# Two experts of a pair spread over interleaved groups of 32 partitions in a mixture-of-experts stage

## The reference, cut to what matters

```
g_idx   = top-1 of 4 groups;  e_idx = top-2 of the 8 experts in that group      # 2 of 32 experts for each token
gate    = softmax prob of the group * softmax over the two selected logits
for each expert e, for its rows xb:   y = (silu(xb @ w_gate[e]) * (xb @ w_up[e])) @ w_down[e]
out[token] += gate * y ;   x = x + out ;   return rmsnorm(x)
```

```
44 50 40 25 15 34 20 12 28 14 21 24 21 25 32 29 | 89 43 53 51 35 47 40 14 7 30 37 29 11 31 48 25
```

## Time and profile before

| | |
|---|---|
| median of 3 runs | 1301.31 us (1301.28 to 1301.44) |
| profiled execution | 1302.32 us, of which the span is 1300.0 us |
| TensorE busy, in the span | 1267.6 us (98%) |
| VectorE / ScalarE / GpSimd busy | 613.1 / 460.4 / 535.5 us |
| moved by DMA | 211.38 MB, mean 163 GB/s |
| mean granted TensorE clock | 0.994 of full speed |

### The profile page before, as it was taken

How to read it: one execution, slowest core, us unless ns; L and a number is a source line. 1 busy time by engine, 2 the same in 40 slices (tenths; PEclk the granted TensorE clock), 3 DMA queues, 4 the chain that set the end, 5 groups by cost and what they waited for, 6 DMA issues and landing times.

```text
span 1300.0 us, 18634 instructions
## 1 busy us (share of the span) xinstructions
PE 1267.6 (98%) x6670; PEld 968.7 (75%) x6670; DVE 613.1 (47%) x1162; ACT 460.4 (35%) x770; POOL 535.5 (41%) x685
## 2 busy tenths in 40 slices
PE   8999999999999999999999999999999999999986
PEld 6767777787888888888888788777888875555552
DVE  4868768725542422222225765757243265222225
ACT  5657534435434324133144534145322210000102
POOL 4633323334555655555545664424644211121100
PEclk9999999999999999999999999999999999999999
DMA  7422222112334433434333333312426989999995
GB/s 221 107 65 56 66 58 66 50 49 81 98 96 113 131 97 97 130 98 129 97 98 114 97 93 85 83 49 67 128 81 268 362 323 394 424 421 424 424 423 240
DMA packets 212157, 211.38 MB, mean 163 GB/s; under 512 B 31903, under 2 KB 193425, under 8 KB 200817
## 3 DMA queue, kind: packets, MB, share of 16 engines
q1 hardware_dynamic: 203104, 200.25, 45.8%
q0 software_dynamic: 5184, 8.29, 1.7%
q10 hardware_dynamic: 3796, 1.86, 0.5%
HBM read 205.76 MB, written 16.78 MB: 171 GB/s over the span
## 4 chain that ended last, share of the span: by engine, by line
issue 39%; POOL 31%; PE 26%; DMA 1%; DVE 1%; POOLq 0%; ACT 0%; SPq 0%; DVEq 0%; ACTq 0%
POOL wlo L661 31%; PE bank L2287 8%; PE bank L2304 4%; PE bank L1915 3%; PE bank L1917 3%; PE bank L1916 3%; PE side L1945 2%; DMA y<-y_rows 1%; PE bank L1956 1%; DMA y_rows<-xe,tabi 1%; PE side L1917 1%; PE side L1915 1%; PE side L1916 1%; PE side L2203 1%; PE bank L2419 0%
## 5 line engine op out<-in xcount | busy, mean ns | idle before, releaser
L661 POOL TENSOR_TENSOR wlo<-raw,whi 128x256 fp32r<-128x256 f32 x644 | 498.2, 805 | 524.4 <-ACT whi L785 524.2
L1916 PE MATMUL bank<-actB_lo,whi 128*128 128x512 f32 x608 | 236.7, 389 | 0.0
L1915 PE MATMUL bank<-actB_hi,whi 128*128 128x512 f32 x576 | 227.7, 395 | 0.5 <-POOL wlo L661 0.5
L1917 PE MATMUL bank<-actB_hi,wlo 128*128 128x512 f32 x576 | 224.4, 390 | 0.0
L785 ACT ACTIVATE whi<-raw 128x1024 fp32r<-128x1024 f32 x161 | 169.0, 1051 | 151.8 <-PE bank L1917 124.9
L1915 PE MATMUL bank<-actA_hi,whi 128*128 128x512 f32 x400 | 157.3, 393 | 0.6 <-DVE actA_lo L1201 0.6
L1916 PE MATMUL bank<-actA_lo,whi 128*128 128x512 f32 x400 | 156.1, 390 | 0.0
L1917 PE MATMUL bank<-actA_hi,wlo 128*128 128x512 f32 x400 | 156.1, 390 | 0.0
L2287 PE MATMUL bank<-gu,xeT 128*64 128x256 f32 x1088 | 127.7, 384 | 4.7 <-issue 2.2
L1916 PEld LDWEIGHTS bank<-actB_lo,whi 128*128 128x128 f32 x608 | 114.2, 188 | 24.1 <-issue 1.0
L1915 PEld LDWEIGHTS bank<-actB_hi,whi 128*128 128x128 f32 x576 | 108.1, 188 | 25.9 <-issue 2.3
(11 more groups left out here) (433 smaller groups left out, 1653.0 us busy)
## 6 DMA issues: line engine op xcount, KB each, us to landing
dn<-in_w_exp_down SPq DMA_DIRECT2D x32, 1024.0 KB, 16.0
raw<-in_w_in SPq DMA_DIRECT2D x57, 512.0 KB, 3.8
gu<-in_w_exp_gate SPq DMA_DIRECT2D x28, 1024.0 KB
gu<-in_w_exp_up SPq DMA_DIRECT2D x28, 1024.0 KB
raw<-in_w_up SPq DMA_DIRECT2D x32, 512.0 KB, 3.9
raw<-in_w_down SPq DMA_DIRECT2D x32, 512.0 KB, 3.6
raw<-in_w_out SPq DMA_DIRECT2D x16, 512.0 KB, 3.7
raw<-in_w_in SPq DMA_DIRECT2D x16, 256.0 KB, 3.1
```

The costliest lines, as they stand in the source:

```text
L661: ins = nc.gpsimd.tensor_tensor(wlo[:, slot, at], raw[:, slot, at], whi[:, slot, at].bitcast(F32), ALU.subtract)
L1915: mm(b[:, :], w_hi, hi[:, k, :], start=first, stop=False)
L1916: mm(b[:, :], w_hi, lo[:, k, :], start=False, stop=False)
L1917: ins = mm(b[:, :], w_lo, hi[:, k, :], start=False, stop=last)
```

## The change

1. The places of the experts of a unit are laid on partitions by groups of 32: expert 0's places 0 to 31 on partitions 0 to 31 and its places 32 to 63 on partitions 64 to 95, expert 1's on 32 to 63 and on 96 to 127 (`QUADRANTS`, `PLACES_OF`). Row numbers, targets and output scales are copied to these partitions in four pieces, where one instruction did it.
2. `rank_at` is filled otherwise: ranks 16o to 16o+15 go one to each of the 16 groups of four neighbouring places, upwards for even o and downwards for odd o.
3. The transposes of the rows write their columns back in the experts' order (`by_expert`), so gates, ups and `hid` stay as they were.
4. The downs are done in four groups of 32 columns, twice as many instructions of half the width.

```diff
+QUADRANTS = ((0, 0), (1, ROWS), (0, 32), (1, ROWS + 32))
+PLACES_OF = tuple((slice(32 * c, 32 * (c + 1)), slice(at, at + 32)) for c, (h, at) in enumerate(QUADRANTS))
+LAST_PLACES = PLACES_OF[-1][0]
+def by_expert(x):
+    return x.rearrange("p (h o s) -> p o h s", h=2, s=32)
...
-            ranks = const("iota")[:, 0:ROWS].rearrange("p (j b) -> p b j", b=8)
-            groups = rank_at.rearrange("p (b o) -> p b o", o=8)
-            for b in range(0, 8, 2):
-                chain(v.tensor_copy(groups[:, b:b + 2, b:8], ranks[:, b:b + 2, 0:8 - b]))
-                if b:
-                    chain(v.tensor_copy(groups[:, b:b + 2, 0:b], ranks[:, b:b + 2, 8 - b:8]))
+            ranks = const("iota")[:, 0:ROWS].rearrange("p (o e) -> p e o", e=16)
+            groups = rank_at.rearrange("p (e o) -> p e o", o=4)
+            for o in range(4):
+                if o % 2 == 0:
+                    chain(v.tensor_copy(groups[:, :, o:o + 1], ranks[:, :, o:o + 1]))
+                else:
+                    chain(v.tensor_scalar(groups[:, :, o:o + 1], ranks[:, :, o:o + 1], -1.0, float(32 * o + 15), ALU.mult, ALU.add))
...
-            chain(v.tensor_scalar(tabi[:, 1, 0:EXTRA_AT], bank[1][:, 0:EXTRA_AT], float(SKIP), None, ALU.add), S("rows_ready"))
+            for to, of in PLACES_OF:
+                ins = v.tensor_scalar(tabi[to, 1, 0:EXTRA_AT], bank[1][of, 0:EXTRA_AT], float(SKIP), None, ALU.add)
+                chain(ins, S("rows_ready") if to == LAST_PLACES else None)
...
-                chain(v.tensor_copy(slotv[:, :, FIRST], bank[2][:, EXTRA_AT:3 * EXTRA_AT].rearrange("p (n c) -> p n c", n=2)),
-                      S("values_listed"))
-                chain(v.tensor_scalar(tabi[:, 0, FIRST], bank[2][:, 0:EXTRA_AT], float(SKIP), None, ALU.add), S("slots_ready"))
+                chain(v.tensor_copy(slotv[:, 0, FIRST], bank[2][:, EXTRA_AT:2 * EXTRA_AT]), S("values_listed"))
+                for to, of in PLACES_OF:
+                    chain(v.tensor_copy(slotv[to, 1, FIRST], bank[2][of, 2 * EXTRA_AT:3 * EXTRA_AT]))
+                for to, of in PLACES_OF:
+                    ins = v.tensor_scalar(tabi[to, 0, FIRST], bank[2][of, 0:EXTRA_AT], float(SKIP), None, ALU.add)
+                    chain(ins, S("slots_ready") if to == LAST_PLACES else None)
...
-                    chain(v.tensor_tensor(tabi[rows, 1, to], slot, back, ALU.add))
-                    chain(v.tensor_copy(tabi[rows, 0, to], slot))
-                    chain(v.tensor_copy(slotv[rows, :, to], table[:, 1:3, :]), S("over_listed") if rows == LOW_ROWS else None)
+                    chain(v.tensor_tensor(back, slot, back, ALU.add))
+                    chain(v.tensor_copy(slotv[rows, 0, to], table[:, 1, :]))
+                    for at, of_ in PLACES_OF if rows == slice(0, P) else ((LOW_ROWS, LOW_ROWS),):
+                        chain(v.tensor_copy(tabi[at, 1, to], prod[of_, 0, EVENS:EVENS + of.stop - of.start]))
+                        chain(v.tensor_copy(tabi[at, 0, to], prod[of_, 0, 0:of.stop - of.start]))
+                        chain(v.tensor_copy(slotv[at, 1, to], late_table(of_, of)[:, 2, :]),
+                              S("over_listed") if rows == LOW_ROWS else None)
...
-                    ins = turn(side[k // 4][:, (k % 4) * P:(k % 4 + 1) * P], xe[:, n_x, :].rearrange("s (p j) -> s j p", j=NK)[:, k, :])
+                    ins = turn(by_expert(side[k // 4][:, (k % 4) * P:(k % 4 + 1) * P]), xe[:, n_x, :].rearrange("s (p j) -> s j p", j=NK)[:, k, :])
...
-                        for h, w in enumerate(weights):
-                            ins = mm(bank[2 + n][ROWS * h:ROWS * (h + 1), :],
-                                     hidT[:, j, k * P + ROWS * h:k * P + ROWS * (h + 1)],
-                                     w[:, k, n * L:(n + 1) * L], start=k == 0, stop=k == 1)
+                        for c, (h, at) in enumerate(QUADRANTS):
+                            ins = mm(bank[2 + n][32 * c:32 * (c + 1), :], hidT[:, j, k * P + at:k * P + at + 32],
+                                     weights[h][:, k, n * L:(n + 1) * L], start=k == 0, stop=k == 1)
```

More of the change, by code:

```diff
@@ L2402, in _ @@
                 for k in range(2):
[L2403 to L2406, removed]
+                    for c, (h, at) in enumerate(QUADRANTS):
+                        ins = mm(bank[2 + n][32 * c:32 * (c + 1), :], hidT[:, LAST_E % 2, k * P + at:k * P + at + 32],
+                                 dn[places_of(LAST_E)[h] % D_BUFS][:, k, n * L:(n + 1) * L], start=k == 0, stop=k == 1)
                 ins.then_inc(S("last_down_done"), 1)
```

## The result

The kernel after the change takes 1304.12 us (median of 20 runs, 1301.87 to 1309.10), the kernel before in the same comparison 1301.57 us (20 runs, 1300.46 to 1303.74). The ratio is 1.0022, with a 95% interval of 1.0013 to 1.0032: 0.22% slower, just past what the measurement tells from no change, 1.5 us above the forecast of 1302.6 and inside its range. The runs after scatter more than those before.

What follows compares the result with a forecast made beforehand. Full DMA engines, half ending late, were taken to set the end, with TensorE close behind. DMA summed to -2.0 us, TensorE to +3.3, less 1.98 slack +1.3 at block 2: 1302.6 us on the median, range 1298.3 to 1305.5.

Steps and rivals of the forecast that it cites:

- The steps between widths: TensorE, changes between gates of 64 and downs of 32 columns: 28 steps at 0.14 us, 3.9 us more.
- rival A: TensorE: steps between 64 and 32 columns are free; 1299.0 us, or 1298 or less with more; chance 0.30.
- rival B: Downs: passes of four groups are longer, up to 8.8 us; 1305.5 us at a third, 1311 in full; chance 0.10.
- Row numbers in four pieces: VectorE before unit 0: three more small chained instructions, all on the path, so unit 0 starts 0.6 us later.
- The waits for weights at units 15 and 16: TensorE's waits of 0.45 and 0.33 us go, as weights now land early enough.
- the 2.19 us before unit 9's gates: TensorE's wait for indirect DMAs issued some units earlier; takes up 0.4 us of the delay, bounds 0 and 1.0.
- `list_overflow` as hidden: VectorE before `y_of(1)`: 23 instructions instead of 10, 2.6 us more, hidden in 3.32 us idle with 0.7 to spare.
- The balance of the engines: DMA engines: rows spread over both halves, 111 each; the late half has 17 less, saving 2.9 us, bounds 0 and 3.7.
- rival C: DMA engines not tied to partitions, so no balance; 1302.6 us, or 1301.9 with free steps; chance 0.10.
- the slack of 1.98: Before block 2 is added: its products are issued 1.98 us before the block is in, covering part of TensorE's delay.
- The sum of TensorE: TensorE's path to block 2: +0.6, +3.9, -0.45, -0.33 and -0.4 give +3.3 us, +1.3 after slack.
- The clock: Lower clock level in unit 15's downs, about 1.7 us, left out of the sum; may stay up or fall elsewhere.

Runs made afterwards that it cites:

- the kernel with only this part: Kernel before with only the downs in four groups of 32 columns, places and lists as they were: 1302.97 us, ratio 1.0008.
- the one without a step between 64 and 32: Kernel after with unit 4's gather not waiting for list_overflow, gates and ups also in groups of 32 columns: 1301.84 us, ratio 1.0001 to before.
- the early gather: Kernel after, unit 4's gather waiting for over_table_full instead of list_overflow's end: 1304.07 us, ratio 1.0011 to before; again 1302.66 us, 1.0001.
- the one with downs of 64: Kernel after with the early gather, but downs again in two groups of 64 columns: 1301.36 us, ratio 0.9991 to before.
- longer lists: Kernel before with only 13 more small chained VectorE copies at the end of list_overflow: 1302.56 us, ratio 1.0002.

## Why the prediction came out as it did

**The steps between widths: right.** 0.14 us for each was forecast, 0.29 us a unit was measured, and the kernel with only this part and the one without a step between 64 and 32 tell them apart from rival A (free steps) and rival B (longer passes). The rule of "TensorEngine Tiling (Array Packing)", Key Properties, in the Trainium skill, that changing the mode drains TensorE and changing the tile does not, agrees with this trace: 12.38 us a unit with steps, 12.08 without.

**Row numbers in four pieces: right, with luck in the number.** The first gates of unit 0 start at 1057.23, 0.64 us later; 0.6 was forecast. But the first of the four pieces itself starts 0.38 us later than the one instruction before (1048.95 after 1048.57), and only 0.26 us are added between it and the gates. Over six executions each, this distance is 7.6 to 8.3 us with one piece and 8.1 to 8.7 with four, 0.4 us more in the mean. The waits for weights at units 15 and 16 are gone, as forecast. Of the 2.19 us before unit 9's gates 0.56 went (0.4 forecast); as this wait is between 0.93 and 2.71 us in the executions of the kernel after with the late and the early gather, that agreement says little.

**`list_overflow` as hidden: this step failed.** The prediction looked at what stands behind it on VectorE, `y_of(1)`, and that was right; of the other reader of its semaphore it said only that "GpSimd's gather of unit 4 comes 2.6 us later and is needed only in unit 2". Needed in unit 2 meant within 8.1 us, and the gather takes 8.1. TensorE waits 2.55 us and loses 1.6 more by the clock. In the time, taking the wait away gives 1.4 and 1.7 us, which is the forecast's miss of 1.5. That this is less than the 4.2 us of the trace fits the wait before unit 9, which with the lower clock behind it shrinks when TensorE is late already; the four executions shown above agree on this. They do not give the 1.5 us themselves: the profiled execution with the early gather stands at 1304.90 us, above the one of the kernel after at 1303.06.

**The balance of the engines: right in kind, mis-sized.** Forecast were 2.9 us less for the late engines. Measured were 2.1 us more for the early ones and 0.4 less for the late ones, since the gap went from 4.9 to 2.5 us instead of to nothing, and since the ends within a half still lie 1.5 to 2.1 us apart. The prediction named the step at one half as the sign of rival C (no balance). It is still there, with half the gap, so neither C nor the forecast came true in full. By the places, the upper half has 113 rows for each engine after the change and the lower 109: 0.7 us, and with the 1.1 us from the place 1.8 of the 2.5. But the eight late engines are here only those that end last; the even rows do not tell which half they serve. Where the 1.1 us come from stays open. This error did not move the time: the last scatter was forecast 2.0 us earlier and landed 0.1 us earlier, but TensorE, 2.46 us later less the slack of 1.98, was still behind it. It would have moved it if the steps had been free.

**The sum of TensorE: near by luck.** Forecast was +3.3 us at block 2, measured +2.46. The late gather with its clock, 4.2 us, was not in the sum. Against it stand three things that were not in it either: the lower clock beside unit 9 (1.6 us) and in unit 15 (1.7 us), which were in the execution before and not in this one, and a wait before the downs of unit 7, which costs 1.1 us in the kernel before and is gone. Timeline of TensorE, before:

```profile
1156.41 3.65 PE L2304 MATMUL bank<-dn,hidT 128*64 128x512 f32 x16 [0.93 <-ACT hidT L1109]
```

The kernel after does not have it in this execution and has it in its second one; what brings it about is open.

**The clock.** The sum left it out, and the scatter goes with it. In the profiled execution the mean granted clock was 0.997 after and 0.994 before; the falls of the earlier trace rows and beside unit 9 did not come, the one in unit 2 did. 0.003 of 1300 us is 3.9 us, which may be why this execution stands 1.1 us below the median of its kernel although the waits are in it. Over the 20 runs of the kernel after, the six with a clock of 0.998 took 1301.87 to 1302.81 us, the seven at 0.994 or less 1304.81 to 1309.10. In this kernel the time goes with the clock; the mean over all its runs, 0.9955, is no lower than that of some faster kernels here (0.9952 for the one with downs of 64).

## What to carry to other kernels

When an instruction gets longer ahead of a semaphore, go through every queue that waits for that semaphore and compare the new time with the landing and not with the issue: here the reader on another engine had no slack, and the one on the same engine, which the prediction looked at, had enough. A step between two widths of column groups on TensorE costs about 0.14 us, so keep one width through a loop, whatever it is. If the DMA engines end unevenly, move a lone expert to the other half of the partitions before making the groups finer; it costs seven small instructions instead of 28 steps. And before a wait is priced by its length, look for a later wait that gets shorter by it: here 4.2 us in unit 2 came back in large part before unit 9.

## What the runs showed of the hardware

Four groups of 32 columns in float32 run fully beside each other: 32 instructions of 512 columns took the 3.43 us of 16 in two groups, if no step stood before or behind them. An indirect DMA's rows go by halves of the partitions to eight engines each: 48 rows as 6 for each of eight engines, 14 as 1 or 2 for each of the others. Where one half has 272 rows of 4 KB more in 200 us of full load, its engines end the weights' stream 4.9 us later. The engines of the upper half seem to fall behind apart from their rows, by 0.2 to 1.1 us in the four executions where the halves can be told apart by their rows. And one wait of 2.2 to 2.8 us on a TensorE that was busy until then was followed in three of three executions (after twice, longer lists once) by about 3.4 us at the lower of its two levels (1.2 instead of 2.4 GHz); the wait of 1.63 us before unit 9 in the profile after was followed by none.
